# Sampled tokens' attention of a decoder step: one score tile per batch, stacked bias rows, key pages in a ring, value pages in two sets

## The reference

```python
D_MODEL, SEQ, DEC_BATCH, DEC_SEQ, PAST_LEN, PAGE_SIZE, N_HEADS, HEAD_DIM = 1024, 1024, 8, 8, 1024, 128, 16, 64

def sample_attention(q, k_new, v_new, logf_new, k_past, v_past, logf_past):
    scale = HEAD_DIM ** -0.5
    cp, cn = jnp.cumsum(logf_past, axis=1), jnp.cumsum(logf_new, axis=1)
    rest = cp[:, -1:, :] - cp
    cn_q = jnp.swapaxes(cn, 1, 2)[..., None]
    s_past = jnp.einsum('bqhd,bkhd->bhqk', q, k_past) * scale
    s_past = s_past + cn_q + jnp.swapaxes(rest, 1, 2)[:, :, None, :]
    s_new = jnp.einsum('bqhd,bkhd->bhqk', q, k_new) * scale
    s_new = s_new + cn_q - jnp.swapaxes(cn, 1, 2)[:, :, None, :]
    s_new = jnp.where(causal, s_new, NEG_INF)
    p = jax.nn.softmax(jnp.concatenate([s_past, s_new], axis=-1), axis=-1)
    return einsum(p[..., :P], v_past) + einsum(p[..., P:], v_new)
# k_past = cache_k[page_table], v_past = cache_v[page_table], logf_past = cache_logf[page_table]
```

## Time and profile before

| | before |
|---|---|
| median of 3 runs | 1947.37 us |
| span of the profiled execution | 1943.1 us |
| what lies around it, median less span | 4.3 us |
| TensorE busy | 1765.1 us (91%) |
| VectorE busy | 885.6 us (46%) |
| ScalarE busy | 721.3 us (37%) |
| mean DMA rate over the span | 83 GB/s |
| DMA rate in the slices of this stage | 307, 265, 269, 327, 276 GB/s |

### The profile page before, as it was taken

The page is one execution under the profiler, slowest core; times in us unless marked ns, Lnnn a source line. Parts: engine busy times, 40 slices in busy tenths (PEclk is TensorE's granted clock), DMA queues, the critical chain, the costliest instruction groups (busy, mean ns, idle before and its releaser), DMA issues.

```text
span 1943.1 us, 33338 instructions
## 1 busy us (share of the span) xinstructions
PE 1765.1 (91%) x11871; PEld 1611.6 (83%) x11871; DVE 885.6 (46%) x1379; ACT 721.3 (37%) x1174; POOL 265.3 (14%) x229
## 2 busy tenths in 40 slices
PE   3699999999999958999999999999779999899997
PEld 2699999999989948888888888888656666699997
DVE  5722222224253374555555556555544444523543
ACT  3311211112043233565656555565533233401432
POOL 1311111110000021222222122222110000000010
PEclk7999999999999979999999999999869999899998
DMA  3011111111211023211101021110318778721102
GB/s 127 23 45 45 47 50 47 45 44 44 72 41 42 8 97 92 57 46 34 56 23 59 19 78 45 34 56 23 132 51 307 265 269 327 276 86 57 41 27 92
DMA packets 163424, 161.57 MB, mean 83 GB/s; under 512 B 18188, under 2 KB 140172, under 8 KB 163126
## 3 DMA queue, kind: packets, MB, share of 16 engines
q1 hardware_dynamic: 163382, 161.03, 24.9%
HBM read 137.20 MB, written 23.80 MB: 83 GB/s over the span
## 4 chain that ended last, share of the span: by engine, by line
PE 73%; DVE 10%; ACT 6%; issue 5%; DVEq 3%; ACTq 2%; POOL 1%; DMA 0%; SPq 0%; POOLq 0%
PE PS L560 14%; PE PS L562 14%; PE PS L561 14%; PE PS L684 4%; PE PS L686 3%; PE PS L685 3%; PE PS L743 3%; PE PS L790 3%; PE PS L731 2%; DVE small L1410 2%; PE PS L857 2%; PE PS L714 2%; PE PS L812 2%; DVE pTl L1421 1%; DVE Hlo L1261 1%
## 5 line engine op out<-in xcount | busy, mean ns | idle before, releaser
L560 PE MATMUL PS<-Hhi,w_hi 128*128 128x364 f32 (+1 forms) x1560 | 519.3, 333 | 58.7 <-DVE Hlo L1261 57.6
L562 PE MATMUL PS<-Hhi,w_lo 128*128 128x364 f32 (+1 forms) x1560 | 515.8, 331 | 0.0
L561 PE MATMUL PS<-Hlo,w_hi 128*128 128x364 f32 (+1 forms) x1560 | 513.4, 329 | 0.0
L560 PEld LDWEIGHTS PS<-Hhi,w_hi 128*128 128x128 f32 x1560 | 297.2, 190 | 66.2 <-issue 44.2
L561 PEld LDWEIGHTS PS<-Hlo,w_hi 128*128 128x128 f32 x1560 | 296.6, 190 | 0.0
L562 PEld LDWEIGHTS PS<-Hhi,w_lo 128*128 128x128 f32 x1560 | 296.1, 190 | 0.0
L684 PE MATMUL PS<-Hhi,w_hi 128*128 128x364 f32 (+1 forms) x768 | 274.0, 357 | 0.1
L686 PE MATMUL PS<-Hhi,w_lo 128*128 128x364 f32 (+1 forms) x768 | 252.4, 329 | 0.0
L685 PE MATMUL PS<-Hlo,w_hi 128*128 128x364 f32 (+1 forms) x768 | 251.8, 328 | 0.0
L490 POOL TENSOR_TENSOR w_raw<-w_raw,GT 128x1024 f32<-128x1024 f32 x65 | 128.6, 1980 | 692.8 <-DMA w_raw<-in_w_kv 383.2
L937 ACT ACTIVATE w_hi<-w_raw 128x1024 fp32r<-128x1024 f32 (+1 forms) x97 | 105.8, 1091 | 293.4 <-PE PS L562 289.4
(11 more groups left out here) (230 smaller groups left out, 2286.3 us busy)
## 6 DMA issues: line engine op xcount, KB each, us to landing
Kpages<-in_cache_k SPq DMA_DIRECT2D x64, 512.0 KB, 5.7
Vpages<-in_cache_v SPq DMA_DIRECT2D x64, 512.0 KB, 5.5
w_raw<-in_w_in_a SPq DMA_DIRECT2D x64, 256.0 KB, 3.0
w_raw<-in_w_ple_gate SPq DMA_DIRECT2D x16, 512.0 KB, 3.7
w_raw<-in_w_kv SPq DMA_DIRECT2D x32, 256.0 KB, 3.1
w_raw<-in_w_in_b SPq DMA_DIRECT2D x32, 256.0 KB, 3.0
parked_x<-X SPq DMA_DIRECT2D x8, 544.0 KB, 5.0
X<-parked_x SPq DMA_DIRECT2D x8, 544.0 KB, 7.7
```

Of the source, the lines that this page charges most:

```text
L560: mm(out, wh, hi[:, k, s:e], start=(k == 0), stop=False)
L561: mm(out, wh, lo[:, k, s:e], start=False, stop=False)
L562: last = mm(out, wl, hi[:, k, s:e], start=False, stop=(k == nk - 1))
```

## The change

One score tile serves a batch. Its 128 rows are the 16 heads x 8 queries, and its 1032 columns the 1024 past keys and the batch's own 8 new keys. The queries of two head pairs share 32 rows (`qc[..., e, 16e:16e+16]`, zeros elsewhere), so that scores are again 8 matmuls of 32x256 for two pages, and the values matmuls put out 256 columns for 32 rows, of which the half that belongs to each head pair is picked at the end by `own`. Biases and mask come from one matmul of 72 stacked rows (`Ar` x `Bk`) for each of three column ranges: key biases high and low, query biases high and low, mask.

The rows of `Bk`, the new values and the queries' bias rows are now loaded by DMA: 5 small ones for each batch (`load_sample`), and 16 once at the start of the stage (`dcn` into `cnA`).

Key pages have 4 places (a ring), value pages two sets of 8 that alternate by batch. While the last head pair still runs, 4 key and 13 value pages are loaded ahead, where before it was 8 key pages. In the loop SyncE loads, for batch b: keys 4 to 7 of batch b+1, then, when the values matmuls of batch b are done, the value pages of batch b+2 and its small rows, with keys 0 to 3 of batch b+2 between the last four value pages.

On TensorE, each batch now starts at page 4; all four first pages of the next batch, its biases and its first scores come before the values matmuls of this one. The loop is unrolled by two. The mask tile `maskQ`, the copies into `vnew`, and the tiles `pick`, `cq`, `cqh`, `cql`, `mq` and `onesr` are gone. In the last batch, `Y` is loaded back once the last biases are done.

```diff
-P_ROUNDS = [(2, 0, 0), (3, 0, 4), (5, 1, 0), (7, 1, 4), (4, 0, PAGES)]
+RING = 4
+NK = KEYS + DS
+R_CN, R_MASK, R_END = 32, 64, 72
...
-        Kr = sb(s2, "Kpages", [P, PAGES, D])
-        RT = sb(s2, "RT", [P, 2, KEYS + NS], F32R)
+        Kr = sb(s2, "Kpages", [P, RING, D])
+        Vb = sb(s2, "Vpages", [P, 2, PAGES, D])
         KT = sb(s2, "KT", [P, 2, NPAIR, 2 * PAGE])
-        pick = sb(s2, "pick", [P, NPAIR, 32], F32R)
-        qc = sb(s2, "qc", [P, NPAIR, 32])
-        cq = sb(s2, "cq", [NS, NPAIR, 32])
-        cqh = sb(s2, "cqh", [NS, NPAIR, 32], F32R)
-        cql = sb(s2, "cql", [NS, NPAIR, 32], F32R)
-        mq = sb(s2, "mq", [NS, 4, 32], BF16)
-        onesr = sb(s2, "onesr", [NS, 512], F32R)
-        Vb = sb(s2, "Vpages", [P, PAGES, D])
-        Ps = sb(s2, "Ps", [P, 2, KEYS + NS])
-        PsT = sb(s2, "PsT", [P, 2, 9, P])
-        Osb = sb(s2, "Osb", [P, 2, P])
+        qc = sb(s2, "qc", [P, 2, 4, 2, 32])
+        knb = sb(s2, "knb", [P, 2, NPAIR, DS])
+        few = sb(s2, "few_rows", [R_CN + 2, 2, D])
+        vb, cnA = few[0:DS, :, :], few[:, 0, :].rearrange("p (b n) -> p b n", b=DB)
+        Ps = sb(s2, "Ps", [P, NK])
+        PsT = sb(s2, "PsT", [P, PAGES + 1, P])
+        Osb = sb(s2, "Osb", [P, P])
+        Ar = sb(s2, "Arows", [R_END, 2, P], F32R)
+        Bk = sb(s2, "Bkeys", [R_END, 2, NK], F32R)
...
+            def load_keys(b, pg, first=False):
+                rows = page(b, pg)
+                if not first:
+                    sp.wait_ge(sems["s_kturn"], 2 * PAGES * b + 2 * (pg - RING) + 2)
+                    sp.sem_inc(sems["sp_step"], 1)
+                sp.dma_start(Kr[:, pg % RING, :], ck[rows, :]).then_inc(sems[f"k_in{pg % RING}"], 16)
+            def load_values(b, par, pg, after=None):
+                rows = page(b, pg)
+                if after is not None:
+                    sp.wait_ge(sems["s_pv"], START["s_pv"] + after + 1)
+                    sp.sem_inc(sems["sp_step"], 1)
+                sp.dma_start(Vb[:, par, pg, :], cv[rows, :]).then_inc(sems[f"v_in{PAGES * par + pg}"], 16)
+            def load_sample(b, par):
+                s_in = sems[f"s_in{par}"]
+                rows = d["rest"][bass.ds(H * b, H)]
+                for x in range(2):
+                    sp.dma_start(f(Bk[H * x:H * x + H, par, 0:KEYS]), rows[:, x, 0:KEYS]).then_inc(s_in, 16)
+                    sp.dma_start(f(Bk[H * x:H * x + H, par, KEYS:]), rows[:, x, bass.ds(KEYS + DS * b, DS)]).then_inc(s_in, 16)
+                sp.dma_start(vb[:, par, :], o["v_sample"][bass.ds(b, 1)].rearrange("b t h d -> (b t) (h d)")).then_inc(s_in, 16)
...
+                    for pg in range(RING):
+                        load_keys(0, pg, first=True)
                     for pg in range(PAGES):
-                        sp.dma_start(Kr[:, pg, :], ck[page(0, pg), :]).then_inc(sems[f"k_in{pg}"], 16)
-                    sp.dma_start(f(RT[:, :, :]), d["rest"]).then_inc(sems["s_restin"], 16)
+                        load_values(0, 0, pg)
+                    for pg in range(5):
+                        load_values(1, 1, pg)
...
-            def value_pages(b):
-                for pg in range(PAGES):
-                    rows = page(b, pg)
-                    if pg == 0:
-                        sp.wait_ge(sems["s_pv"], START["s_pv"] + b)
-                        sp.sem_inc(sems["sp_step"], 1)
-                    sp.dma_start(Vb[:, pg, :], cv[rows, :]).then_inc(sems[f"v_in{pg}"], 16)
-            with sp.Fori(0, DB - 1) as b:
-                value_pages(b)
-                for pg in range(PAGES):
-                    rows = page(b + 1, pg)
-                    sp.wait_ge(sems["s_kturn"], 16 * b + 2 * pg + 2)
-                    sp.sem_inc(sems["sp_step"], 1)
-                    sp.dma_start(Kr[:, pg, :], ck[rows, :]).then_inc(sems[f"k_in{pg}"], 16)
+            with nc.allow_non_contiguous_dma(reason="eight values of each head, once"):
+                for x in range(2):
+                    for b in range(DB):
+                        sp.dma_start(cnA[R_CN + x:R_CN + x + 1, b, :].rearrange("x (h t) -> x h t", t=DS),
+                                     dcn[:, x, DS * b:DS * b + DS].rearrange("(x h) t -> x h t", x=1)).then_inc(sems["s_cnin"], 16)
+                sp.wait_ge(sems["s_ones"], 1)
+                load_sample(0, 0)
+                load_sample(1, 1)
+                for pg in range(RING, PAGES):
+                    load_keys(0, pg)
+                for pg in range(5, PAGES):
+                    load_values(1, 1, pg)
+                for pg in range(RING):
+                    load_keys(1, pg)
+                def feed_batch(b, par, keys=True):
+                    for pg in range(RING, PAGES):
+                        load_keys(b + 1, pg)
+                    for pg in range(PAGES):
+                        load_values(b + 2, par, pg, b if pg == 0 else None)
+                        if pg == 0:
+                            load_sample(b + 2, par)
+                        if pg >= PAGES - RING:
+                            load_keys(b + 2, pg - RING)
+                with sp.Fori(0, 3) as i:
+                    for par in range(2):
+                        feed_batch(2 * i + par, par)
+                for pg in range(RING, PAGES):
+                    load_keys(DB - 1, pg)
...
-            value_pages(DB - 1)
+            sp.wait_ge(sems["s_all"], DB)
...
-            def s_biases(b):
-                pe.wait_ge(sems["s_prep"], b + 1)
-                pe.wait_ge(sems["s_pt0"], START["s_pt0"] + 3 * b)
-                pe.wait_ge(sems["s_pt1"], START["s_pt1"] + 2 * b)
-                for s_ in range(2):
-                    for c in range(2):
-                        s_bias(b, s_bank(s_, c), s_, 512 * c, 512)
+            def s_bias(b, par):
+                pe.wait_ge(sems["s_prep"], b + 1)
+                pe.wait_ge(sems[f"s_in{par}"], 40 * (b - par) + 80)
+                pe.wait_ge(sems["s_exp"], START["s_exp"] + b)
+                for c0, n in ((0, 512), (512, 512), (KEYS, DS)):
+                    mm(SS[:, c0:c0 + n], Ar[:, par, :], Bk[:, par, c0:c0 + n], start=True, stop=False)
+                for e in range(2):
+                    for g_ in range(4):
+                        last = mm(PS[32 * g_:32 * g_ + 32, 4, 0:DS], qc[:, par, g_, e, :], knb[:, par, 2 * g_ + e, :], start=False, stop=(e == 1))
...
-                        for g_ in range(4):
-                            i = 4 * s_ + g_
-                            k, v = (P, Vb[:, pg, i * P:(i + 1) * P]) if pg < PAGES else (NS, vnew[:, i * P:(i + 1) * P])
+                    for g_ in range(4):
+                        k, v = (P, Vb[:, par, pg, 256 * g_:256 * g_ + 256]) if pg < PAGES else (DS, vb[:, par, 256 * g_:256 * g_ + 256])
+                        last = mm(PS[32 * g_:32 * g_ + 32, 7, 0:256], PsT[0:k, pg, 32 * g_:32 * g_ + 32], v, start=(pg == 0), stop=(pg == PAGES - 1))
...
+            def sample_batch(b, par, first=False, more=True):
+                k_turn(b, 4)
+                k_turn(b, 5)
+                if not first:
+                    s_y_turn(b - 1)
+                s_scores(b, par, 1)
+                k_turn(b, 6)
+                k_turn(b, 7)
+                s_scores(b, par, 2)
                 if more:
                     k_turn(b + 1, 0)
+                s_scores(b, par, 3)
                 if more:
+                    for pg in range(1, 4):
+                        k_turn(b + 1, pg)
+                s_p_turn(b, 0)
+                s_p_turn(b, 1)
+                if more:
+                    s_bias(b + 1, 1 - par)
+                    s_scores(b + 1, 1 - par, 0)
+                s_p_turn(b, 2)
+                s_values(b, par)
...
+                act.wait_ge(sems["s_max"], b + 1)
+                af(Ps[:, :], SS, ACT.Exp, bias=small[:, 0:1], accum_out=small[:, 1:2])
+                act.drain().then_inc(sems["s_exp"], 1)
                 if more:
+                    for pg in range(1, 4):
+                        keep_keys(b + 1, pg)
...
+            ve.wait_ge(sems["s_cnin"], 32 * DB)
+            prepare(0, 0)
+            for pg in range(4):
                 keep_keys(0, pg)
```

More of the change, by code:

```diff
@@ L806, in s_scores @@
-            def s_scores(b, pp, pairs=range(NPAIR)):
+            def s_bias(b, par):
[7 more added lines that the diff above has]
+                        last = mm(PS[32 * g_:32 * g_ + 32, 4, 0:DS], qc[:, par, g_, e, :], knb[:, par, 2 * g_ + e, :], start=False, stop=(e == 1))
+                last.then_inc(sems["s_all"], 1)
@@ L808, in s_scores @@
+            def s_scores(b, par, pp):
                 for c in range(2):
                     pe.wait_ge(sems[f"s_kt{c}"], 1 + PAGES * b + 2 * pp + 2)
[L810 to L815 removed]
@@ new lines, in s_scores, with s_p_turn @@
+                last.then_inc(sems["s_score"], 1)
+            def s_p_turn(b, r):
+                if r == 0:
+                    pe.wait_ge(sems["s_exp"], START["s_exp"] + b + 1)
+                if r == 1:
```

(59 more changed lines are left out.)

226 lines of the change are left out of this document (62 added, 164 removed).

## The result

The changed kernel takes 1972.87 us (median; 1972.03 to 1975.46), the kernel before 1947.21 beside it: the ratio is 1.0136, with a 95% interval of 1.0124 to 1.0148. It is slower by 1.4%. The forecast was 1966, slower. The profiled execution has a span of 1970.2 us, 27.1 more than before.

The account below looks back on a forecast made before the run. SyncE's queue, landing key pages 0 to 3 late, with a lowered clock, was to set a 32.6 us period. 10 + 6 x (32.6 - 29.33) - 11.2 = +18.4 us: span 1961.5, time 1966 us, range 1945 to 1985.

Parts of the forecast that it names:

- The queue sets the period: SyncE's loads: key page 3 lands 21.6 us after the values end, 9.1 us of work follow; period 30.7 us at full clock.
- The clock: TensorE waits for key page 0, its clock falls to half in every batch, and the period becomes 32.6 us, bounds 30.7 and 35.5.
- the two cases: Batch period with the clock lowered once, 31.8 us, or again in the gap between pages 1 and 2, 34.3 us.
- clock kept: Rival: short pieces of work hold TensorE's clock up, period 30.7 us, +7 us, 1954 us; chance 0.13.
- TensorE alone: TensorE's work per batch is 19.4 us plus 3.4 us of waits; 22.8 us if nothing else were late.
- The start: Start of the stage: first batch's values end near 1491.7 instead of 1481.8, +10 us, bounds +7 and +14.
- the price of the 16 tiny loads: SyncE at the start of the stage: 16 tiny loads at 0.42 us each, 6.7 us, from 4.5 to 9.6.
- The first batch then takes 23.7 us: After the first scores end near 1468, the first batch takes 23.7 us, its values ending near 1491.7.
- The end: The last batch waits for no next page and takes 18.5 us instead of 29.7: -11.2 us, bounds -12 and -10.
- The signs: Profile after: period 32 to 33 us, DMA waits ahead of page 0 and page 2 or 3, DMA share below 0.7.
- The rival that the lookahead holds: Key page 3 lands within 14 us of the values' end, period 22.8 us, -40 us, 1907 us; chance 0.12.
- The price named against this rival: SyncE's queue: 11 pages must land in 14 us, 1.0 us a page, where the fullest window has 1.26.

Follow-up runs that it names:

- E9: The changed kernel with added identity turns on TensorE in two waits of batches 1 to 6, 66 ahead of key page 0 and 17 ahead of page 2: 1960.25 us.
- E4: The changed kernel without the value page loads of batches 2 to 7; keys, small loads and arithmetic stay: 1917.74 us, a single run.
- E3: The changed kernel with one load of the queries' bias rows instead of sixteen at the start of the stage: 1968.35 us.
- E7: E6 with the single bias-row load of E3, key pages 4 to 6 of batch 0 issued ahead of the small loads, and VectorE copying between set-up steps: 1914.42 us.
- E6: The changed kernel with key page i and value page i issued in turn, key first, and the small loads after the fourth pair: 1923.78 us.
- E5: The changed kernel with 50 added identity turns on TensorE in the wait for key page 0, batches 1 to 6: 1972.94 us.
- E8: E7 with ScalarE's copy of key page 1 moved ahead of its wait for the maximum: 1912.25 us.
- E10: The changed kernel with added identity turns, 60 ahead of key page 0 and 17 ahead of page 2, and small loads behind key page 3: 1951.71 us.

## Why the prediction was right, and where it was not

**The queue sets the period: right.** Key page 0 was put at T + 8.4 and its landing at T + 14.0; it was issued at T + 9.1 and landed at T + 14.8. Page 3 was to land at T + 21.6 and did so at T + 22.4. The difference is the small loads, with which the second value page comes 4.0 us behind the first where 3.2 had been put, and landings of 5.7 to 6.0 us for 5.6. Behind page 3's landing the prediction put 9.1 us; in E9 it is 8.2. That the sum comes out, 30.7 at full clock forecast and 30.5 measured, is in part luck: these two errors, of nearly a microsecond each, cancel.

**The clock: right in kind, and its size between the two cases.** The prediction had 31.8 for one lowering and 34.3 for two, and took 32.6, 1.9 above the full clock; E9 gives 1.8 to 1.95. Page 0's turn takes 1.96 or 1.97 us in all six batches, after waits of 7.2 to 7.7 us, and the scores behind it 1.94 in four and 1.57 and 1.65 in the first two. Whether the gap of 2 us ahead of page 2 lowers it again was left open. It does in some batches: page 3's turn and the first probabilities take 1.97 and 1.61 us in the batches of 33.10 and 33.15 us, and 1.20 and 1.04 in those of 31.71 and 31.66. So the mean of 32.7 is a mixture of batches with one lowering, just where the prediction had them, and of batches with two, and how many there would be of each was not worked out. The rival *clock kept* (1954) is excluded by these rows. The Trainium skill, "TensorE: Matmul & The Clock Gate", section "HAM oscillation — how this bites in real kernels", says that a kernel which waits for DMA between bursts of matmuls falls back again and again. The trace agrees, though only the first period (34.06) comes near the 34.3 that a full second lowering was to cost. The wait in the trace before on which the prediction rests here was for ScalarE's exponential and not for a DMA, and it is not true that this trace has no wait as long as 7 us: TensorE waits 14.0 us for VectorE near the start of the program, outside this stage.

**TensorE alone: right.** E4 has 22.8 and 23.0 in the batches at full clock for the 22.8 that were worked out, and 23.5 in the mean. TensorE is busy for 19.05 us of the one of 22.78, where the sum was 19.4. (The terms given for the work before add up to 26.45 and not to 26.7; nothing hangs on it.)

**The start: mis-sized.** This term was +10 with bounds of +7 and +14, and it measured +18.1, of which 1.2 us come from ahead of the stage. The first step that failed is the price of the 16 tiny loads, taken at 0.42 each: they are 0.63 apart, just outside the 0.28 to 0.6 of the nearest rows, 10.1 us for 6.7. The first scores hide most of that: they end at 1469.0 where 1468 was foretold, because copies and scores behind the loads take 7.6 us (1461.4 to 1469.0) and not 10. But the delay goes on through the queue. Key pages 4 to 7 are issued from 1465.8, 4.4 us later than thought (3.4 by the price, 0.9 because the first tiny load goes out at 1450.1 and not at 1449.2), and keys 0 to 3 of batch 1 from 1473.75, the first of them landing 7.2 us later at 1481.0. The second step that failed is "The first batch then takes 23.7 us", a batch without a wait for key page 0: TensorE waited 3.5 us for it, the clock fell, and the batch took 30.9. E3 and E7 recover 5.6 and 9.7 us of this term. How the rest divides was not taken apart. This one term is the whole miss: the span was forecast at 1961.5 and is 1970.2, 8.7 us more, of which 8.1 are the start. The time misses by only 6.9, because the 4.3 us that the prediction put between span and median are 2.7 in the runs after.

**The end: right.** -11.1 for -11.2, with the first 40 values matmuls behind the gap at the lower clock (4.05 us for 2.37).

**The signs.** Two did not come. A DMA share below 0.7 was foretold for the stage; it is 0.74. And in the six batches after the change no page turn behind page 0 waits for a DMA: the wait foretold ahead of page 3 shows in E9, where the lowered clock no longer hides it.

**The rival that the lookahead holds (1907)** had the right mechanism, for another order of the same loads. Its condition, page 3 landed by T + 14, fails after the change by 8.4 us. In E6 key page 3 is issued at T + 8.5 and lands at T + 14.3 (T = 1550.78, issue at 1559.32, landing 5.8 later), and the time is 1923.8. The price named against this rival, 11 pages in 14 us, held only for the order of the change. The Trainium skill's rule in "DMA: Bandwidth & Descriptors", section "Rules for kernel authors", to issue early and wait late, is kept by the value pages, and it is just these that make the keys late.

## What to carry to other kernels

Loads that share one in-order queue are best asked for in the order of their due times (here 32.7 us a batch in one order and 24.5 in another); a second buffer for one stream lets it run ahead, and whatever is issued early stands in front of what is urgent. Before buying a deeper buffer, write the queue's order with a time for each issue and read where the next due load stands. A small load costs nearly half as much of the issuing engine as a large one here (0.5 us and 1.2), so put small loads behind the urgent ones or merge them.

An experiment that fills a wait with dummy work must fill every gap of the path, or the lowered clock only moves to the next piece (E5 against E9).

## What was not expected of the hardware

- Sixteen loads, each of 16 runs of 32 bytes into one partition, are issued 0.63 us apart (10.07 us for the sixteen); one load of the same numbers takes a single 0.28 us issue, in E3 and E8.
- The time from issue to landing of a 512 KB page grows with what is queued: 3.2 us on an empty queue, 6.0 in a batch after the change, 7.2 at the start of its stage, 7.6 in E10.
- With keys and values in turn the queue kept 341 GB/s over 150 us, at a DMA share of 0.95; before, 293 GB/s at 0.78.
